# A kernel of two transformer blocks on one core: another timetable for the extra work of the first 35 slots, and the first input issued ahead of the small transfers

## The reference, cut to what matters

```python
def _modulate(x, g, shift, scale):
    return _rms(x, g) * (1 + scale) + shift
...
        h_lat = _modulate(x, norm_mix_g[layer], sh1, sc1)
        h_ctx = _modulate(ctx, norm_mix_g[layer], csh1, csc1)
...
        x = x + g1 * y_lat
        x = x + g2 * _peer(_modulate(x, norm_ffn_g[layer], sh2, sc2), ...)
```

## Time and profile before

| | us |
|---|---|
| median of 3 runs (lowest, highest) | 1635.02 (1633.87, 1635.48) |
| the profiled execution | 1635.06 |
| its span | 1633.3 |
| TensorE busy | 1339.8 |
| VectorE busy | 782.6 |
| ScalarE busy | 452.3 |
| GpSimd busy | 318.7 |

### The profile page before, as it was taken

The page is one execution under the profiler, slowest core; times in us unless marked ns, Lnnn a source line. Parts: engine busy times, 40 slices in busy tenths (PEclk is TensorE's granted clock), DMA queues, the critical chain, the costliest instruction groups (busy, mean ns, idle before and its releaser), DMA issues.

```text
span 1633.3 us, 19079 instructions
## 1 busy us (share of the span) xinstructions
PE 1339.8 (82%) x7112; PEld 770.1 (47%) x7112; DVE 782.6 (48%) x1899; ACT 452.3 (28%) x1235; POOL 318.7 (20%) x272
## 2 busy tenths in 40 slices
PE   6999999998877887779798887699996676667666
PEld 4476886796434554335354542287841221221122
DVE  3102774437786776788887787626420010100001
ACT  2121214313344343454544443225210000000001
POOL 0000000004444434444455445202000000000000
PEclk9999999999999999799999999999998987887888
DMA  8467326929999999999999999854589999999997
GB/s 371 196 276 296 144 108 276 419 106 388 404 411 408 406 424 420 422 397 408 417 420 421 421 421 421 362 209 188 220 360 426 428 428 427 427 429 427 429 428 303
DMA packets 62577, 583.53 MB, mean 357 GB/s; under 512 B 6944, under 2 KB 7328, under 8 KB 8864
## 3 DMA queue, kind: packets, MB, share of 16 engines
q1 hardware_dynamic: 23904, 302.99, 44.9%
q0 software_dynamic: 36864, 268.45, 40.0%
q10 hardware_dynamic: 1728, 11.03, 1.7%
HBM read 581.39 MB, written 1.05 MB: 357 GB/s over the span
## 4 chain that ended last, share of the span: by engine, by line
PE 42%; DMA 38%; DVE 12%; ACT 4%; issue 2%; POOL 1%; SPq 0%; ACTq 0%; DVEq 0%; PEldq 0%; POOLq 0%
PE ps L1145 38%; DMA slab<-w_stream 18%; DMA big<-peer_uv,big 16%; DVE big L2319 5%; DMA big<-w_stream 2%; DMA scratch<-w_stream 2%; PE ps L1414 1%; POOL big L717 1%; PE ps L1422 1%; ACT big L971 1%; ACT big L967 1%; DVE big L2330 1%; DVE big L2267 1%; ACT big L963 0%; ACT L963 0%
## 5 line engine op out<-in xcount | busy, mean ns | idle before, releaser
L1145 PE MATMUL ps<-big 128*128 128x512 f32 (+2 forms) x2054 | 614.2, 561 | 176.8 <-ACT big L971 121.8
L1145 PEld LDWEIGHTS ps<-big 128*128 128x128 f32 (+1 forms) x2054 | 256.4, 176 | 486.3 <-ACT big L971 210.8
L717 POOL DMA_INDIRECT big<-peer_uv,big x256 | 307.8, 1202 | 734.7 <-DVE big L2362 370.0
L2319 DVE CUSTOM_DVE_ANT_0 big<-big 128x1024 f32<-128x1024 f32 x256 | 310.5, 1224 | 125.8 <-DMA big<-peer_uv,big 120.5
L1145 PE MATMUL ps<-xh,slab 128*128 128x128 f32 (+1 forms) x1152 | 170.0, 306 | 0.0
L1145 PEld LDWEIGHTS ps<-xh,slab 128*128 128x128 f32 x1152 | 158.8, 194 | 20.4 <-issue 12.7
L1145 PE MATMUL ps<-slab,big 128*32 128x512 f32 x752 | 118.8, 762 | 59.5 <-DMA slab<-w_stream 58.0
L963 ACT ACTIVATE big<-big 128x1 f32<-128x1 f32 x256 | 51.4, 201 | 331.3 <-DVE big L2319 330.9
L2573 DVE TENSOR_TENSOR big<-big,ps 128x512 f32<-128x512 f32 x8 | 5.5, 687 | 222.3 <-PE ps L1145 222.3
L1145 PEld LDWEIGHTS ps<-slab,big 128*32 128x32 f32 x752 | 24.1, 127 | 144.9 <-DMA slab<-w_stream 85.7
L1103 ACT ACTIVATE big<-ps,mod,gain 128x128 f32<-128x128 f32 x32 | 12.0, 456 | 288.2 <-PE ps L1145 288.2
(11 more groups left out here) (380 smaller groups left out, 1244.8 us busy)
## 6 DMA issues: line engine op xcount, KB each, us to landing
slab<-w_stream SPq DMA_DIRECT2D x87, 2048.0 KB, 15.8
big<-w_stream SPq DMA_DIRECT2D x35, 2048.0 KB, 32.8
scratch<-w_stream SPq DMA_DIRECT2D x8, 2048.0 KB, 32.4
slab<-w_stream SPq DMA_DIRECT2D x12, 1024.0 KB, 24.3
scratch<-w_stream SPq DMA_DIRECT2D x8, 1024.0 KB, 31.8
big<-w_stream ACTq DMA_DIRECT2D x2, 2048.0 KB, 14.9
big<-peer_uv,big POOLq DMA_INDIRECT x256, 11.3
big<-w_stream SPq DMA_DIRECT2D x2, 1024.0 KB, 6.0
```

Of the source, the lines that this page charges most:

```text
L717: nc.gpsimd.indirect_dma_start(out=uv[b], out_offset=None, in_=peer_uv, in_offset=bass.IndirectOffsetOnAxis(ap=idxu[:, s:s + 1], axis=0)). ...
L1145: ins = nc.tensor.matmul(*a, **kw)
L2319: V.tensor_tensor_reduce(out=u, in0=u, in1=xtok, scale=1.0, scalar=0.0, op0=ALU.mult, op1=ALU.add, accum_out=dots[:, s:s + 1]).then_inc(do ...
```

## The change

It has two parts. At the start, the input is the first DMA that SyncE issues; cond, the first constants and the columns are issued by ScalarE at the head of its list, and ScalarE's first ada copy stands ahead of the root of norm 0. In the slots, query 2 of tile 0 moves from slot 4 to 7 and its scores from 7 to 10, the search of head 2 moves from slots 9, 14, 17, 21 to 13, 15, 17, 21, the late output tiles from 2, 8, 9, 10 to 9, 13, 16, 18, two residuals by two slots each, norm 3 by one or two slots on each engine, and the context's issue from slot 18 to 22.

```diff
--- before.py
+++ after.py
@@ -125,7 +125,7 @@
 def query_at(t, m):
 
     if t == 0:
-        return (-6, 0)[m] if m < 2 else 16 * m - 28
+        return (-6, 0, 7)[m] if m < 3 else 16 * m - 28
     return (42, 46, 58, 62, 74, 78, 90, 100)[m]
 
 
@@ -133,9 +133,9 @@
     return query_at(t, m) + (1 if t == 0 and m < 2 else 3)
 
 
-OUT_AT = (None, None, None, None, 2, 8, 9, 10)
+OUT_AT = (None, None, None, None, 9, 13, 16, 18)
 XTOK_AT = ((-4, -3), (118, 119))
-RESIDUAL_AT = ((12, 16, 20, 23), (138, 141, 144, 147))
+RESIDUAL_AT = ((12, 16, 22, 25), (138, 141, 144, 147))
 CTX_KEYS_AT = (126, 131, 141, 147)
 KEYS_AT = (160, 165)
 VALUES_AT = (170, 176)
@@ -172,6 +172,8 @@
 
     if n == 1:
         return (4, 5, 6, 7)
+    if n == 2:
+        return (13, 15, 17, 21)
     s = (n - 1) * TOPK
     return (s - 7, s - 2, s + 1, s + 5)
 
@@ -575,10 +577,7 @@
                     sp.wait_ge(slab_used, value)
                 sp.dma_start(slab[slot][:, :], w_stream[n]).then_inc(slab_loaded[slot], 16)
 
-            sp.dma_start(conds[:, :], cond).then_inc(cond_loaded, 16)
-            first = slice(0, N_CONST_FIRST)
-            for dst, src in ((cst[:, first], consts[:, first]), (col[:, :], cols), (xT[:, :], x_t)):
-                sp.dma_start(dst, src).then_inc(x_loaded, 16)
+            sp.dma_start(xT[:, :], x_t).then_inc(x_loaded, 16)
             low, high = slice(0, SLAB // 2), slice(SLAB // 2, SLAB)
             load(0, 0, None)
             load(1, 1, None)
@@ -750,6 +749,10 @@
                 ins.then_inc(act_step, 1)
                 act.wait_ge(act_step, steps[0])
 
+            act.dma_start(conds[:, :], cond).then_inc(cond_loaded, 16)
+            first = slice(0, N_CONST_FIRST)
+            for dst, src in ((cst[:, first], consts[:, first]), (col[:, :], cols)):
+                act.dma_start(dst, src).then_inc(x_loaded, 16)
             act.wait_ge(cond_loaded, 16)
             nc.scalar.activation(conds[:, :], conds[:, :], ACT.Silu).then_inc(cond_ready, 1)
 
@@ -781,8 +784,8 @@
                 for k in range(4 * half, 4 * half + 4):
                     norm_shift(i, k, h[:, k * T:(k + 1) * T], modc(0, 0, k, i))
 
+            ada_row(0, big[:, 0:T])
             norm_root(0)
-            ada_row(0, big[:, 0:T])
             ada_row(1, big[:, 0:T])
             shift_half(0, 0)
             norm_root(1, r=rstd_c)
@@ -984,10 +987,10 @@
                             query_out(t, m)
                         if s - 2 == scores_at(t, m) and query_at(t, m) >= 0:
                             scores_out(t, m)
-                if s == 18:
+                if s == 22:
                     act.wait_ge(y_filled, 2 * KD)
                     act.dma_start(hcT[:, :], ctx2_t).then_inc(ctx2_loaded, 16)
-                if s == 29:
+                if s == 31:
                     norm_root(3, P)
                 if s in (33, 35):
                     for j in range(4):
@@ -1607,7 +1610,7 @@
                             key_scores(tq, m)
                 if s in OUT_AT:
                     late_out(OUT_AT.index(s))
-                if s == 26:
+                if s == 28:
                     norm(3, P)
                 if s in XTOK_AT[1]:
                     early_turn(1, XTOK_AT[1].index(s))
@@ -2403,10 +2406,10 @@
                 if s in RESIDUAL_AT[0]:
                     j = 2 * RESIDUAL_AT[0].index(s)
                     residual_tile(1, 1, range(j, j + 2), 3, 2, by_half(6), lambda j: KD + j // 4 * 4 + 4)
-                if s == 28:
+                if s == 30:
                     norm_open(3, colv("g_ffn"), modp(0, 4), P)
-                if s in (31, 32, 34, 35):
-                    j = 2 * (31, 32, 34, 35).index(s)
+                if s in (32, 33, 34, 35):
+                    j = 2 * (32, 33, 34, 35).index(s)
                     norm_scale(3, xT, hT, range(j, j + 2), P, P)
                 if s == 114:
                     norm_open(4, colv("g1"), modp(1, 1, 1))
```

## The result

| | before | after |
|---|---|---|
| median of 6 runs, us (lowest, highest) | 1635.61 (1633.87, 1640.36) | 1645.04 (1644.27, 1647.32) |
| the profiled execution, us | 1635.06 | 1646.59 |

The changed kernel is slower by 9.4 us. The ratio is 1.0056, with a 95% interval of 1.0041 to 1.0071, that is 6.7 to 11.6 us.

A forecast was written before the change was run, and what follows sets the result against it. A chain of waits bounds the start, and DMA bounds the slots, with TensorE freeing row buffers late from 394 to 421 us. 1635.06 + 8.6 - 0.7 - 1.0 - 0.5 = 1641.5 us, range 1631.5 to 1645.5.

The forecast's parts named there:

- The late columns: Start: ScalarE's small packets alternate with SyncE's large ones, so VectorE's squares start at 17.1 instead of 8.46, +8.6 us.
- Both prices of a shared packet: Start: constants and columns beside slabs cost 5.2 and 5.1 us by bytes, about 6 each by the profile rows.
- The swap: Start: first ada copy ahead of norm 0's root cuts TensorE's idle time from 1.16 to 0.50 us, -0.66 us.
- Rivals 1 and 3: Start: small transfers slip through, 1631.9 us, chance 0.14; whole transfers alternate, +3.4 us on VectorE, 1636.3 us, chance 0.13.
- The slots: Expert-row slots: the new timetable wins back part of 4.0 us of lost DMA time, -1.0 us.
- The walk: Slots, TensorE step by step: gather 12 goes 5 us earlier, gather 15 5.4 us after gather 14, gather 24 unmoved.
- Norm 3: Late slots: VectorE's 1.77 us wait for sums is covered, but scalings crowd into slots 32 to 35; -0.5 us.
- rival 4: Slots: query before slot 8, wait at slot 13 and crowded norm cost 2 us, 1645.0 us; chance 0.08.
- Rival 2: Slots: the timetable regains all 4.0 us of DMA time and the 1.8 us wait, 1637.2 us; chance 0.12.

The follow-up runs named there:

- e5_ctx_before_slabs: Kernel before with only the change's start, but the context issued ahead of slabs 0 and 1: 1642.22 us against 1636.20 for the kernel before, ratio 1.0034.
- e11_change_small_behind_x: Changed kernel, but constants and columns issued behind x on SyncE's queue, only cond on ScalarE: 1635.92 us against 1636.53 for the kernel before, ratio 0.9996.
- e2_slots_only: Kernel before with the change's whole slot timetable and the old start: 1637.85 us against 1636.34 for the kernel before, ratio 1.0007.
- e8_norm_only: Kernel before with only norm 3 moved (sums at slot 28, opening 30, root 31, scalings 32 to 35): ratio 1.0008 to the kernel before.
- e3_swap_only: Kernel before with only the first ada copy put ahead of norm 0's root: 1635.27 us against 1636.34 for the kernel before, ratio 0.9993.

## Why the prediction was right

The forecast was 1641.5 us; it came out slower, as forecast, at 1645.04, inside the range, and 3.5 us above the number.

- **The late columns: right in mechanism and size.** This is the cause of the loss. Forecast landings were 6.5 for cond (2.0 + 3.1 + 1.4), 11.7 for the constants and 16.8 for the columns; the issues and their durations give 0.74 + 5.9 = 6.6, 1.19 + 10.7 = 11.9 and 1.67 + 15.4 = 17.1. The squares started at 17.09, forecast 17.1. Both prices of a shared packet in the prediction, by bytes and by the rows further down, rest on one-for-one alternation, and the byte price was the right one. e5_ctx_before_slabs shows that the partner's packet size sets it, and e11_change_small_behind_x that nothing else in the start costs anything measurable. One small term is off: by the prediction's own rates x was through at 5 + (1.51 - 0.73)/0.426 = 6.8, not 6.9, and was seen at 8.4, so the time from the bytes to the landing is 1.6 and not 1.4. With it the sum is 17.0.
- **The swap: right where it was forecast.** 0.50 us of idle time in front of the turn in every profile that has it; first key matmul at 31.35, forecast 31.4. The start as a whole: +7.92 at dot 0, forecast +7.9. Whether the swap costs something at slot 0 instead is open (last section).
- **Rivals 1 and 3: out.** VectorE's start would have been before 8.46 by the one and near 11.9 by the other. By the Trainium skill ("DMA: Bandwidth & Descriptors", Queues, rings and completion order) an engine drains a packet of typically 9 to 17 descriptors before it switches; counted in the packets that this profile lists, the rows show 242 against 243 and 178 against 177, one for one. The constants and columns landed after 10.7 and 15.4 us, so a whole small transfer did not pass in one turn, and for this case the measurement decides. Whether a packet of the profile is the page's packet or one of its descriptors, no run here shows.
- **The slots: this step failed.** "The lost 4.0 us can't all come back: bounds 0 and -4.0; I take -1.0". The term came out at nothing or a little above: e2_slots_only measures +1.1 us (-1.0 to +3.4) for the whole timetable, where -1.5 was forecast with norm 3. The walk itself was nearly right: gather 12 came 4.9 us sooner in e2_slots_only (forecast 5; 3.2 in the profile after, whose slot 0 was slow), gather 24 no sooner, and the gap between gathers 14 and 15 was 5.3 us after and 5.7 in e2_slots_only (forecast 5.4). VectorE's wait at slot 13 was undersized: 4.73 in e2_slots_only, 3.05 in the profile after, forecast 2.5. What was wrong was to give 375 to 385 GB/s to a stretch that contains this gap; it moved 362 in both. The lead won before the gap was lost in it, 0.81 MB against 0.83, and 0 was the bound that my own unmoved gather 24 spoke for.
- **Norm 3: wrong in its small term.** The wait of 1.77 us for the sums was to be covered. It is still 1.41 in the profile after, and there is a new one of 1.18 for the root. e8_norm_only ends at 1.0008 (0.9993 to 1.0023), so -0.5 is neither shown nor excluded.
- **What is left.** 9.4 - 7.9 = 1.5 us lie outside the start. e2_slots_only's 1.1 would fit them, but so would the slow slot 0, and neither is shown to be the reason. The measured 1645.04 is the number of rival 4 (1645.0), the timetable that costs 2 us, and not mine. Whether the timetable truly costs isn't shown, since its interval includes zero; that it gives the 1.5 us of the forecast lies outside the interval. Rival 2, a gain of 5.8, is out. The time fell 0.5 us below the upper end of the stated range, and just above the forecast's own range of 1639 to 1645; that it fell inside is in part luck. Of the 3.5 us by which I missed, 0.55 are the base: the sum was made on 1635.06, and the six runs before have a median of 1635.61, over 1633.87 to 1640.36.

## What to carry to other kernels

Before moving a small transfer to another queue to free a sequencer, look at what the first queue moves meanwhile: with packets taken in turn, the small one's time is its number of rows times the sum of both packet sizes, over the DMA rate. Here 1.4 us of issues saved made the first wait end 8.6 us later. Put small transfers that a first wait needs ahead of the large ones, in the same queue. When extra work is rearranged between slots, find the slot that another engine holds fixed (here dot 8, behind a look-up); TensorE's lead of 0.8 MB of gathered rows ended there. A change to that engine's list might carry it past; no run tried that.

## What the runs showed of the hardware

- A transfer of 128 rows of 536 B took 3.7 us to land where its own queue moved it ahead of larger ones, 5.4 behind a 1 MB input in the same queue, 13.0 beside a queue of mixed 8 KB and 16 KB packets, and 15.4 beside 16 KB packets throughout.
- TensorE's clock makes single profiles of the same schedule differ. In the profile after, the granted clock was 0.66 from 390.0 to 392.5 us, and slot 0's four matmuls took 3.68 us and not 1.98, behind the same idle time of 1.92 us as before. One profile is therefore no measure of a timetable whose parts are worth 1 to 2 us.
- The slow slot 0 may not be chance. Slot 0's four matmuls took 2.77 to 3.68 us in all seven profiles of kernels with the swap (e3_swap_only, which changes nothing else, among them: 2.94), and 1.98 in all six without it, always behind an idle time of 1.9 us but for e8_norm_only (0.28, with a slower stretch just ahead). It moves dot 8, counted from dot 0, from about 25.5 to 27.1 us. So it goes with the swap and not with the slots' timetable. Why a swap at 17 us should show at 380 us, no run shows, and at the end it can't be seen: e3_swap_only's ratio is 0.9993 (0.9974 to 1.0011).
